# Attention probabilities are divided by their sum on VectorE before they are transposed, instead of the attention output after it

## The reference, cut to what matters

```python
s = jnp.einsum('bnqhgd,bnkhd->bhgnqk', qb, kb)
s = jnp.where(mask, s, -jnp.inf)
m = jnp.maximum(jnp.max(s, axis=-1, keepdims=True), sink)
p = jnp.exp(s - m)
denom = jnp.sum(p, axis=-1, keepdims=True) + jnp.exp(sink - m)
probs = p / denom
out = jnp.einsum('bhgnqk,bnkhd->bnqhgd', probs, vb)
...
x = x + (g_pool * a + g_attn * out) @ w_out
```

## Time and profile before

| what | value |
|---|---|
| runs | 1464.11 us median of 3 (1462.46 to 1471.2) |
| the profiled execution's own time | 1459.95 us |
| its span from first to last instruction | 1458.1 us |
| busy share of the span: PE, PEld | 95%, 76% |
| busy share: DVE, ACT, POOL | 61%, 27%, 57% |
| granted TensorE clock, mean | 0.975 of full |

### The profile page before, as it was taken

The page is one execution under the profiler, slowest core; times in us unless marked ns, Lnnn a source line. Parts: engine busy times, 40 slices in busy tenths (PEclk is TensorE's granted clock), DMA queues, the critical chain, the costliest instruction groups (busy, mean ns, idle before and its releaser), DMA issues.

```text
span 1458.1 us, 19719 instructions
## 1 busy us (share of the span) xinstructions
PE 1382.9 (95%) x6923; PEld 1115.3 (76%) x6923; DVE 891.7 (61%) x1274; ACT 398.1 (27%) x757; POOL 837.2 (57%) x651
## 2 busy tenths in 40 slices
PE   5898889989699999999999999999799999999998
PEld 4676768878378888888877888767588888888887
DVE  5676488763666666674018789745675888887000
ACT  3431223332422222211013202355423233232000
POOL 1233334425466666667775677432267777777664
PEclk9889999989899999999999999999999999999999
DMA  9356222212123333345332232211032333333332
GB/s 354 128 187 216 59 58 49 68 44 64 39 80 93 101 100 89 100 128 172 94 111 61 85 101 87 73 56 47 26 98 85 96 101 101 87 100 93 91 94 83
DMA packets 224459, 142.05 MB, mean 97 GB/s; under 512 B 5611, under 2 KB 211088, under 8 KB 224400
## 3 DMA queue, kind: packets, MB, share of 16 engines
q1 hardware_dynamic: 221333, 136.45, 31.2%
q10 hardware_dynamic: 3067, 4.78, 1.0%
HBM read 139.12 MB, written 2.10 MB: 97 GB/s over the span
## 4 chain that ended last, share of the span: by engine, by line
PE 83%; DVE 8%; issue 4%; ACT 2%; POOL 2%; DMA 0%; POOLq 0%; SPq 0%; DVEq 0%; ACTq 0%
PE ps L553 25%; PE ps L554 24%; PE ps L555 24%; PE ps L845 2%; DVE norm_acc L1698 1%; POOL w_lo L516 1%; PE ps L1088 1%; PE ps L1104 1%; PE ps L1117 1%; DVE SS L1991 1%; ACT h_hi L1198 1%; PE ps L639 1%; DVE xT L2162 1%; POOL w_hi L513 1%; DVE h_lo L1719 1%
## 5 line engine op out<-in xcount | busy, mean ns | idle before, releaser
L516 POOL TENSOR_TENSOR w_lo<-raw,w_hi 128x1024 fp32r<-128x1024 f32 x213 | 535.1, 2512 | 17.8
L553 PE MATMUL ps<-h_hi,w_hi 128*128 128x512 f32 x1064 | 427.3, 402 | 12.7 <-DVE h_lo L1719 7.1
L554 PE MATMUL ps<-h_lo,w_hi 128*128 128x512 f32 x1064 | 418.9, 394 | 0.0
L555 PE MATMUL ps<-h_hi,w_lo 128*128 128x512 f32 x1064 | 418.7, 394 | 0.0
L512 POOL TENSOR_TENSOR w_hi<-raw,cst 128x16 fp32r<-128x16 f32 x213 | 63.3, 297 | 573.6 <-PE ps L555 515.4
L553 PEld LDWEIGHTS ps<-h_hi,w_hi 128*128 128x128 f32 x1064 | 202.2, 190 | 65.9 <-issue 18.8
L555 PEld LDWEIGHTS ps<-h_hi,w_lo 128*128 128x128 f32 x1064 | 202.4, 190 | 43.5
L554 PEld LDWEIGHTS ps<-h_lo,w_hi 128*128 128x128 f32 x1064 | 202.7, 190 | 39.7
L513 POOL TENSOR_SCALAR w_hi<-raw 128x1008 fp32r<-128x1008 f32 x213 | 232.8, 1093 | 0.0
L2080 DVE SCALAR_TENSOR_TENSOR f_acc<-ps,par,f_acc 128x441 f32<-128x441 f32 (+2 forms) x176 | 122.3, 695 | 50.3 <-ACT f_acc L1198 27.9
L553 PE MATMUL ps<-f_hi,w_hi 128*128 128x512 f32 x352 | 138.4, 393 | 0.5 <-POOL w_lo L516 0.5
(11 more groups left out here) (301 smaller groups left out, 1944.3 us busy)
## 6 DMA issues: line engine op xcount, KB each, us to landing
raw<-in_w_up SPq DMA_DIRECT2D x88, 512.0 KB, 3.7
raw<-in_w_in SPq DMA_DIRECT2D x59, 512.0 KB, 3.7
raw<-in_w_down SPq DMA_DIRECT2D x32, 512.0 KB, 3.7
ada_first<-in_w_ada SPq DMA_DIRECT2D x8, 1024.0 KB, 10.2
raw<-in_w_out SPq DMA_DIRECT2D x16, 512.0 KB, 3.6
v_tok<-in_w_ada SPq DMA_DIRECT2D x14, 512.0 KB, 6.1
raw<-in_w_down SPq DMA_DIRECT2D x16, 384.0 KB, 3.3
ada<-in_w_ada SPq DMA_DIRECT2D x10, 512.0 KB, 5.4
```

The source lines that it names most:

```text
L516: pool.tensor_tensor(w_lo[:, slot % 2, :], raw[:, slot, :], w_hi[:, slot % 2, :].bitcast(F32), ALU.subtract).then_inc(S("lo_split"), 1)
L553: nc.tensor.matmul(dst, lhs_hi, rhs_hi, start=first, stop=False)
L554: nc.tensor.matmul(dst, lhs_hi, rhs_lo, start=False, stop=False)
L555: return nc.tensor.matmul(dst, lhs_lo, rhs_hi, start=False, stop=last)
```

## The change

The reciprocal is taken for each step's four heads, and VectorE multiplies the exponentials in `scores_sb` with it, in place, one `tensor_scalar` per head, while queries still lie on partitions. TensorE transposes the scaled probabilities: each head's transposes wait for that head's multiplication (`probs_scaled`) instead of for the exponentials. `spread_shares`, `copy_shares`, the tile `share` and its bank are gone; `outputs` multiplies with 0.5 alone. ScalarE takes the sinks' exponentials in every step (4 heads) and no longer in every second (8 heads).

```diff
@@ tensor: turn_probs, spread_shares, the loop
-            pe.wait_ge(S("probs_ready"), 4 * s + 4)
             if s >= 1:
                 pe.wait_ge(S("pt_copied"), 2 * s)
             for i in range(4):
-                if i == 2 and s >= 2 and s % 2 == 0:
-                    pe.wait_ge(S("share_copied"), s // 2)
+                pe.wait_ge(S("probs_scaled"), 4 * s + i + 1)
                 for half in halves(n):
...
-        def spread_shares(half):
-            pe.wait_ge(S("share_ready"), half + 1)
...
-            for k in range(4):
-                for odd in range(2):
-                    h = 8 * (half % 2) + 2 * k + odd
-                    mm = nc.tensor.matmul(ps[odd * HD:(odd + 1) * HD, share_bank(half), k * P:(k + 1) * P],
-                                          stat[:, h:h + 1].broadcast_to([P, HD]), const("ident", P), start=True, stop=True)
...
-            if s and s % 2 == 0:
-                spread_shares(s // 2 - 1)
             if s + 1 < STEPS:
                 scores(s + 1)
             turn_probs(s)
-            if s == STEPS - 1:
-                spread_shares(2 * BLOCKS - 1)
@@ scalar
-            if s % 2:
-                act.wait_ge(S("sink_offset"), s // 2 + 1)
-                part = att_stat[:, n % 2, 3, 8 * (s // 2 % 2):8 * (s // 2 % 2) + 8]
-                activate(part, part, ACT.Exp).then_inc(S("sink_part"), 1)
+            act.wait_ge(S("sink_offset"), s + 1)
+            activate(stat(s, 3), stat(s, 3), ACT.Exp).then_inc(S("sink_part"), 1)
...
-            if s and s % 2 == 0:
-                copy_shares(s // 2 - 1)
             copy_probs(s)
@@ vector
+        def weights(s):
+            n, g = s // 4, s % 4
+            stat, hs = att_stat[:, n % 2], slice(4 * g, 4 * g + 4)
+            keys = slice(0 if n else P, 2 * P)
+            dve.wait_ge(S("probs_ready"), 4 * s + 4)
+            dve.wait_ge(S("sink_part"), s + 1)
+            link(vec.tensor_tensor(stat[:, 2, hs], stat[:, 2, hs], stat[:, 3, hs], ALU.add))
+            link(vec.reciprocal(stat[:, 4, hs], stat[:, 2, hs]))
+            for i in range(4):
+                t = scores_sb[:, (s % 2) * 4 + i, keys]
+                vec.tensor_scalar(t, t, stat[:, 4, 4 * g + i:4 * g + i + 1], None, ALU.mult).then_inc(S("probs_scaled"), 1)
...
-            vec.scalar_tensor_tensor(qT[...], ps[:, 6 + i, :]..., 0.5, share[:, i, :]..., ALU.mult, ALU.mult)
+            vec.tensor_scalar(qT[...], ps[:, 6 + i, :]..., 0.5, None, ALU.mult)
@@ vector, the loop
-            if s and s % 2 == 0:
-                shares(s // 2 - 1)
             if s + 1 < STEPS:
                 maxima(s + 1)
+            weights(s)
             if s and s % 2 == 0:
                 outputs(s // 2 - 1)
```

More of the change, by code:

```diff
@@ L189, in build_program @@
                 ("ada_acc_1", [P, 512], F32)],
-               [("kd", [P, BLOCKS, 2 * P], F32), ("v2", [P, BLOCKS, P], F32), ("pt_sb", [P, 2, 512], F32),
-                ("share", [P, 2, 512], F32)])
+               [("kd", [P, BLOCKS, 2 * P], F32), ("v2", [P, BLOCKS, P], F32), ("pt_sb", [P, 2, 512], F32)])
     M = {}
@@ L225, in build_program @@
     sb("region_mixers_and_ffn", [P, 96 * 256])
-    norm_sq, norm_acc, norm_root, norm_rinv, norm_t, g_e, g_z, g_att, g_qe, ada_acc_1, kd, v2, pt_sb, share = N.values()
+    norm_sq, norm_acc, norm_root, norm_rinv, norm_t, g_e, g_z, g_att, g_qe, ada_acc_1, kd, v2, pt_sb = N.values()
     hc_hi, hc_lo, ys_hi, ys_lo, p1, p2, yg_hi, yg_lo = (M[k] for k in (
@@ L391, in pool_unit @@
         return FIRST["pool"] + p if p < 4 else FIRST["pool_late"] + p - 4
-    def share_bank(half):
-        return 1 if half == 2 * BLOCKS - 1 else 5
     def gate_parts(s):
@@ L1621, in copy_probs @@
                 activate(v(pt_sb[:, i, :]), v(ps[:, 4 + i, :]), ACT.Copy).then_inc(S("pt_copied"), 1)
-        def copy_shares(half):
-            act.wait_ge(S("share_spread"), half + 1)
-            if half >= 2:
-                act.wait_ge(S("o_scaled"), half - 1)
-            activate(share[:, half % 2, :], ps[:, share_bank(half), :], ACT.Copy).then_inc(S("share_copied"), 1)
         def y2_high(k):
@@ L1639, in _ @@
                 y2_high(1)
-            if s and s % 2 == 0:
-                copy_shares(s // 2 - 1)
             copy_probs(s)
-            if s == STEPS - 1:
-                copy_shares(2 * BLOCKS - 1)
             if s and gate_done_in(s - 1):
@@ L2271, in maxima @@
             vec.tensor_scalar(stat[:, 1, hs], stat[:, 0, hs], -1.0, None, ALU.mult).then_inc(S("max_negated"), 1)
[L2272 to L2282 removed]
+            dve.wait_ge(S("max_negated"), s + 1)
+            vec.tensor_tensor(stat[:, 3, hs], sinks[:, hs], stat[:, 1, hs], ALU.add).then_inc(S("sink_offset"), 1)
+        def weights(s):
[4 more added lines that the diff above has]
+            dve.wait_ge(S("sink_part"), s + 1)
             link(vec.tensor_tensor(stat[:, 2, hs], stat[:, 2, hs], stat[:, 3, hs], ALU.add))
[L2284 removed]
+            link(vec.reciprocal(stat[:, 4, hs], stat[:, 2, hs]))
+            for i in range(4):
+                t = scores_sb[:, (s % 2) * 4 + i, keys]
+                vec.tensor_scalar(t, t, stat[:, 4, 4 * g + i:4 * g + i + 1], None, ALU.mult).then_inc(S("probs_scaled"), 1)
         def outputs(half):
             n, i = half // 2, half % 2
[L2289 removed]
             dve.wait_ge(S("weighed"), 2 * half + 2)
[L2291 to L2292 removed]
+            vec.tensor_scalar(qT[:, 4 * i:4 * i + 4, n * P:(n + 1) * P], ps[:, 6 + i, :].rearrange("p (k t) -> p k t", k=4), 0.5,
+                              None, ALU.mult).then_inc(S("o_scaled"), 1)
         def pool_gated(k):
@@ L2327, in _ @@
                 attention_gated(slice(0, 4), slice(2 * P, T)).then_inc(S("y2_sum"), 1)
-        shares(2 * BLOCKS - 1)
         order.wait()
```

19 lines of the change are left out of this document (removed).

## The result

The changed kernel takes **1528.4 us** (median of 4 runs, 1525.3 to 1531.3) beside 1464.44 us for the kernel before (4 runs, 1462.46 to 1471.2): ratio 1.0434, 95% interval 1.041 to 1.0458. It is 64 us slower. The forecast was 1522, inside a range of 1496 to 1542. The profiled execution took 1531.3 us, of which 1529.5 are its span.

A forecast was written before the change was run, and what follows sets the result against it. TensorE, full in the attention stage's middle, was taken as the bound. The profiled 1459.95 us + 37.8 of net stalls + 22 of clock gave 1519.8, stated as 1522 against the median; range 1496 to 1542.

The forecast's parts named there:

- The stall of a wide step: TensorE, steps with 256 keys: idle from the scores' end to the first transpose, waiting for VectorE's multiplication, 2.91 us.
- The loss of a step: TensorE, steps with 256 keys: transposes end at 3.93 us behind the scores instead of 0.85, 3.08 us lost.
- for 128 keys: Steps 1 and 2: shorter maxima and multiplications make the loss 2.6 us instead of 3.08.
- Steps 0 and 1: Start of the attention stage: 1.3 us lost in step 0, 4.4 in step 1, with 1.8 of GpSimd blocking.
- GpSimd in steps 4, 7 and 10: Weight splits on GpSimd hold up VectorE's negation inside the stall, 0.8 us in each, 2.4 in all.
- The tail: From step 13's transposes to the first projection matmul: later divisions on VectorE cost +2.3 us net of both spreads.
- The sum without the clock: Attention stage: stalls, GpSimd and tail less 6.1 us of removed spreads give +37.8 us.
- The clock: Granted clock falls to half behind 11 of 13 stalls in steps 1 to 13, 2.0 us each, +22 us.
- (1): Attention stage: the stalls come but the clock stays, 1498 or 1502 us; chance 17%.
- (2): Attention stage: longer clock falls or more blocking by GpSimd, +38 + 44, 1542 to 1546 us; chance 11%.
- (3): Attention stage: multiplications are hidden and TensorE only loses its spreads, 1453 us, faster; chance 2%.
- (4): Attention stage: the order costs less, through overlapping maxima or a later stage making it good, 1470 us; chance 2%.

The follow-up runs named there:

- Experiment 5: The changed kernel with VectorE's weights of step s (sum, reciprocal, multiplications) moved ahead of the maxima of step s + 1: 1468.88 us, ratio 1.0049.
- experiment 3: The changed kernel with GpSimd's splits of the attention stage's ten weight units cut to 16 columns, their other weights left out: 1513.85 us.
- experiment 1: The changed kernel with useless matmuls filling TensorE's stalls, 12 in steps 3 to 14, 9 in steps 1 and 2: 1501.33 us.
- experiments 2 and 8: Changed kernel with 5 useless matmuls per stall: 1507.09 us; weights-first kernel with start and tail mended, 1473.08, or start alone, 1466.48.
- experiment 9: The kernel before, with multiplications in steps 4 to 13 alone, each step's weights ahead of the next maxima on VectorE: 1455.1 us, ratio 0.9957.
- experiment 6: The changed kernel with the next step's scores ahead of the first gate part on TensorE, VectorE's order kept: 1495.03 us.

## Why the prediction was right, and where its terms were off

**The cause holds.** VectorE's queue put the division behind the maxima of the next step, and TensorE had nothing to do meanwhile. Experiment 5 moves that one call and takes back 56 to 60 of 64 us.

**The stall of a wide step** was put at 2.91 us and is 2.98. Maxima to sinks took 990.48 to 992.50, 2.02 (2.03 in the sum); sum and reciprocal 0.41 (0.42); from the first multiplication to the transposes 0.50 (0.35 and 0.06: the signal took 0.15). The multiplication of 256 columns takes 0.348 us (0.35 from the bracket of 0.17 to 0.48), that of 128 columns 0.280. The loss of a step, 5.01 - 1.92 = 3.09, was put at 3.08. Two workings were looser than their results: the rows give an overlap of neighbours of 0.06, (4 x 481 - 1740) / 3 ns, not 0.08; and for 128 keys the subtraction as written, 3.08 - 0.54 - 0.28, gives 2.26 and not 2.6, since it leaves out that the transposes against which the loss is counted are shorter too (0.41 from 943.58 to 943.99 before). With that, step 2 lost 2.55: a stall of 2.38 and transposes of 0.58.

**Steps 0 and 1.** Step 0 begins its transposes 7.00 us behind the first scores in place of 5.66, +1.34 (1.3 said). That this agrees is luck: 0.64 of it is a negation of 1.96 us beside a split, which the term did not have, and without splits (experiment 3) only 0.70 is left. From there to step 1's it is 9.85 in place of 5.50, +4.35 (4.4 said), of which the negation held up by a split is 1.76 (1.8 said).

**GpSimd in steps 4, 7 and 10** adds 3.78 - 2.98 = 0.80 each, as the sum has it (0.8). What the sum left out hangs on it. Its GpSimd terms are 5.0 us in all, with the 0.8 of step 13 that stands in its tail. Experiment 3 has 5.6 of idle time for them and 5.3 of clock beside it by the traces; the whole is 14.6 by the medians, 13.7 by the ratios.

**The tail.** Its term begins where the sum's other terms end, at the end of step 14's scores, so step 13's stall lies in it. From there to the projection the kernel before takes 17.5 us (1023.66 to 1041.19) and the changed one 24.15 (1088.39 to 1112.54): +6.6, where the prediction said +2.3. Nearly all of it ran at half the clock, by the stretch view of the changed kernel from within step 13's stall on:

```profile
1090.30:1112.54 22.24, 13.67 (x56) 8.18 (x56) 16.28 (x45) 10.38 (x29) 0.82 (x1) 0.50 0.08 24
```

In experiment 1, where the same waits stand, most of them filled, and the clock is at 0.50 only for the last 2.2 us, this stretch takes 20.0 (1062.74 to 1082.78), +2.5. So the chain of the tail was sized about right, and the other 4.1 are the clock. Half of the 13.67 would be more, 6.8, but not all of that comes back at full clock: TensorE is then earlier and waits longer, 2.54 instead of 1.65 in front of step 15's transposes.

**The sum without the clock** was 37.8. Measured, the stage's idle time grew by 44.0 and the spreads gave back 8.2: 35.8, 2 less.

**The clock** is the term that was mis-sized. It was put at 11 falls of 2.0, +22; the busy time says +29.3. In steps 1 to 12 of the profiled execution each stall, twelve of twelve, went with a stretch at 0.5, seven of them 3.4 us long and five 6.8, such as this one of step 8:

```profile
1028.90:1035.70 6.80, 5.79 (x22) 4.19 (x22) 2.85 (x9) 3.86 (x12) 1.21 (x2) 0.50 0.01 2
```

It begins 1.0 us before the stall ends. So did six of the twelve begin inside their stall, where the prediction has the fall come behind it. These low stretches of the twelve steps are 58.0 us together, of which some 7 lie in the stalls and cost nothing; the other 51 held work that needs half of that at full clock, 25, or 2.1 for each fall. The remaining 4 are the tail, which the sum had given at most one fall of 2.0. So the cost of one fall was right; there were more of them, and the last one did not end before the projection. Behind step 0's stall of 3.37 us the clock did not fall:

```profile
935.08:938.45 3.37, 0.00 (x0) 0.03 (x1) 2.65 (x17) 1.74 (x9) 0.27 (x1) 1.00 0.51 148
938.45:943.60 5.15, 5.15 (x25) 3.45 (x27) 4.65 (x10) 2.40 (x11) 0.00 (x0) 1.00 0.02 7
```

That is one execution again: the same stall of 3.37 us in step 0 was followed by a fall in experiment 1 (at 933.85), and in experiments 2 and 8.

**The rivals.** (1), the clock stays, is refuted by the experiments that filled the stall, and with it the reading of the Trainium skill's page TensorE: Matmul & The Clock Gate (Seeing it yourself) as a rule that a gap needs 5.2 us: by this trace the stalls of 2.4 to 4.1 us in steps 1 to 13 each went with a fall, so it does not agree. (2), longer falls, was the direction of the error, though its 44 were not reached. (3) was right that the cover is there, and experiment 9 uses it; in the kernel as changed the queue kept it out of reach. Of (4) nothing is seen: 35.8 us of the 37.8 came.

**What failed behind the prediction** is my expectation that the better order alone would beat the kernel before (experiment 5). I had looked at the steady steps only. At both ends VectorE is the engine that others wait for (seven gated sums at the start, the wide ones in step 15), and there the kernel that divides by spreads was the faster one. The reason I see is that VectorE needs only a sum and a reciprocal for it; that is argued from the queue, and no run takes it apart.

## What to carry to other kernels

When work is moved to an engine with much idle time, look first at what it will be queued behind: here VectorE had half its time free and the move cost 64 us, because one call stood behind a wait for the very engine that was waiting. Price a stall of the bottleneck engine with the clock behind it (2.1 us on top of 3 here), and check it by filling the stall. Ask of each stage separately which engine is late: the only kernel here that still divides and was faster than the old one, by 0.43% (0.26 to 0.59%), does it on VectorE in ten steps and through TensorE in six. No other mixture was tried.

## What the runs showed of the hardware

**A split on GpSimd holds up some instructions of VectorE and not others.** Held until an instruction of the split ended were the negation of 128x4 (0.17 alone, 0.97 and up to 1.96), the sum of 128x4 (0.16 alone, 1.72) and the first of the multiplications, SBUF to SBUF (four in 1.14 alone, 3.03). Not held were the product that reads PSUM (0.68 beside a split) and the reciprocal of 128x4, though it reads and writes SBUF (0.18, from 965.62 beside the split that starts at 965.59 in experiment 6). It works the other way too: in experiment 5 GpSimd's 128x16 instruction, 0.22 elsewhere, took 0.99 beside the last of the gated sums, which have two inputs in SBUF as well, and ended 0.10 behind it (941.20 and 941.10). The Trainium skill, SBUF — State Buffer (SBUF: two separate sides), says that VectorE and GpSimd share a pair of ports as an exclusive lock, for VectorE's two-port modes and for its instructions with two inputs in SBUF. The trace agrees: the sum, which was held, has two inputs in SBUF and the product, which was not, has one, and the negation and the sum ended 0.03 us behind the split. That the negation and the multiplications run in a two-port mode is not shown by the trace.

**Useless matmuls made a kernel faster**, by 22 to 27 us of 1528: 12 of them in a stall of 3 us kept the granted clock at 1.00 for 133 us. Five, with 1.5 us left idle, did nearly as well (1507.09 beside 1501.33).
